# Low-rank layers and preparation of the recurrence moved beside the convolved projection; layer 1's modulation moved into the first feed-forward

## The reference

```python
cs = silu(c)
for l in range(2):
    mod = cs @ ada_w[l] + ada_b[l]          # 1024 x 6144: shifts, scales, gates of layer l
    h = rmsnorm(x, g) * (1 + sc1) + sh1
    if l == 0:
        z = h @ mix_in                      # 4*512 columns r, k, v, u and 3*512 of the attention
        r, k, v, u = split(dwconv3(z[..., :2048], mix_conv))
        g = sigmoid(u @ g1) @ g2
        kk = k * k_k;  kk = kk * rsqrt(sum(kk*kk, per head) + eps)
        for d in range(2):                  # two directions
            w = decay(w0[d] + tanh(u @ w1[d]) @ w2[d])
            a = sigmoid(a0[d] + (u @ a1[d]) @ a2[d])
            kd = k * (1 + (a - 1) * k_a)
            y += wkv7_scan(r, w, kd, v, kk, a)
            bonus += sum(r * kd * r_k, per head) * v
    ...
    h = rmsnorm(x) * (1 + sc2) + sh2
    y = (gelu(gate) * val) @ down           # gate, val = split(dwconv3(h @ up)), 2 * 2816 columns
```

## Time and profile before

| | |
|---|---|
| median of 3 runs | 3074.9 us (3071.58 to 3075.23) |
| profiled execution, its own time | 3071.72 us |
| its span, first to last instruction | 3069.9 us |
| PE busy | 2658.7 us, 87% of the span |
| DVE busy | 1577.3 us, 51% |
| ACT busy | 1129.5 us, 37% |
| POOL busy | 979.2 us, 32% |

### The profile page before, as it was taken

One profiled execution on the slowest core, in us unless ns is written; L12 is line 12 of the kernel. 1 busy time (PEld: TensorE's weight loads), 2 busy tenths in 40 slices (PEclk: granted clock), 3 DMA queues, 4 the chain that ended last, 5 costly groups with the idle time before them and its releaser, 6 DMA issues. The chain is left out here.

```text
span 3069.9 us, 55055 instructions
## 1 busy us (share of the span) xinstructions
PE 2658.7 (87%) x23104; PEld 2154.1 (70%) x23104; DVE 1577.3 (51%) x2253; ACT 1129.5 (37%) x1774; POOL 979.2 (32%) x660
## 2 busy tenths in 40 slices
PE   2698997965789989558899999999778899999998
PEld 1576775731789889347688888877556688888887
DVE  4463664503555454416555556445626555556445
ACT  2211224523434333224344444445324344444434
POOL 0411111003212111142577775000131577775000
PEclk9799998987899999769899999999879899999999
DMA  4555745046311310332222223754032222223654
GB/s 167 161 179 175 240 171 149 16 148 245 93 44 47 83 44 4 117 118 83 70 84 85 85 83 131 245 170 148 30 96 83 75 88 85 83 83 135 236 187 143
DMA packets 301852, 361.14 MB, mean 118 GB/s; under 512 B 31652, under 2 KB 227585, under 8 KB 301613
## 3 DMA queue, kind: packets, MB, share of 16 engines
q1 hardware_dynamic: 291966, 351.38, 35.1%
q10 hardware_dynamic: 9648, 6.34, 0.6%
HBM read 282.12 MB, written 75.55 MB: 117 GB/s over the span
## 5 line engine op out<-in xcount | busy, mean ns | idle before, releaser
L2401 POOL TENSOR_TENSOR cg_u_lo<-cg_u_raw,cg_u_hi 128x512 fp32r<-128x512 f32 x216 | 329.3, 1533 | 136.4 <-ACT cg_u_hi L2287 136.4
L304 PE MATMUL cg_ps<-m_hi,cg_u_hi 128*128 128x512 f32 x844 | 331.3, 393 | 33.0 <-POOL cg_u_lo L2401 28.7
L306 PE MATMUL cg_ps<-m_hi,cg_u_lo 128*128 128x512 f32 x844 | 330.8, 392 | 0.0
L305 PE MATMUL cg_ps<-m_lo,cg_u_hi 128*128 128x512 f32 x808 | 316.0, 391 | 0.0
L2287 ACT ACTIVATE cg_u_hi<-cg_u_raw 128x512 fp32r<-128x512 f32 x216 | 132.1, 629 | 386.5 <-PE cg_ps L306 234.1
L304 PEld LDWEIGHTS cg_ps<-m_hi,cg_u_hi 128*128 128x128 f32 x844 | 159.9, 189 | 68.2 <-POOL cg_u_lo L2401 29.5
L304 PE MATMUL cg_ps<-over_y_tx,cg_u_hi 128*128 128x512 f32 x480 | 186.7, 389 | 0.0
L305 PE MATMUL cg_ps<-over_y_tx,cg_u_hi 128*128 128x512 f32 x480 | 186.7, 389 | 0.0
L306 PE MATMUL cg_ps<-over_y_tx,cg_u_lo 128*128 128x512 f32 x480 | 186.7, 389 | 0.0
L306 PEld LDWEIGHTS cg_ps<-m_hi,cg_u_lo 128*128 128x128 f32 x844 | 159.7, 189 | 33.6
L2451 DVE SCALAR_TENSOR_TENSOR cg_z<-cg_ps,top_conv_f,cg_z 128x1023 f32<-128x1023 f32 x88 | 112.9, 1283 | 133.8 <-ACT cg_z L2311 133.8
(11 more groups left out here) (416 smaller groups left out, 6691.8 us busy)
## 6 DMA issues: line engine op xcount, KB each, us to landing
cg_u_raw<-in_ffn_up SPq DMA_DIRECT2D x88, 512.0 KB, 5.3
cg_u_raw<-in_ffn_down SPq DMA_DIRECT2D x64, 512.0 KB
za_mw<-in_ada_w SPq DMA_DIRECT2D x12, 2048.0 KB
over_f_d_raw<-in_ffn_down SPq DMA_DIRECT2D x48, 512.0 KB
scr_act<-cg_z SPq DMA_DIRECT2D x44, 512.0 KB, 2.7
qkv_mw<-in_ada_w SPq DMA_DIRECT2D x8, 2048.0 KB
mod_w<-in_ada_w SPq DMA_DIRECT2D x8, 1024.0 KB
za_w_raw<-in_mix_in SPq DMA_DIRECT2D x16, 512.0 KB, 4.3
```

The lines of the kernel that those rows point to most:

```text
L304: nc.tensor.matmul(out, a_hi, b_hi, start=first, stop=False)
L305: nc.tensor.matmul(out, a_hi, b_lo, start=False, stop=False)
L306: return nc.tensor.matmul(out, a_lo, b_hi, start=False, stop=last)
L2401: G.tensor_tensor(u_lo[:, n % RING], source(g, i), u_hi[:, n % RING].bitcast(F32), ALU.subtract).then_inc(ulo_done, 1)
```

## The change

`project_convolved` becomes `project_and_prepare`. It makes the tiles in the order u0..u3, k0..k3, r0, v0, r1, v1, r2, v2, r3, v3, keeps them in SBUF, and between the tiles runs what the two low-rank stages did, on a pair of PSUM buffers `pr` that the small products take in turn (`ORDER`). Both low-rank stages and their loads from DRAM are gone; the stores of z and of the results stay. Two weight buffers are left of four. The loops are written out.

```diff
-            project_convolved(nc, a["mix_in"], consts["conv_a"], h_hi, h_lo, scr["z"], a["ada_w"], a["ada_b"], scr["mod"], consts)
+            project_and_prepare(nc, a["mix_in"], consts["conv_a"], h_hi, h_lo, a["rwkv_w1"], a["rwkv_a1"], a["rwkv_g1"], a["rwkv_w2"],
+                                a["rwkv_a2"], a["rwkv_g2"], tab, consts, scr["z"], scr["lw"], scr["aa"], scr["kk"], scr["bon"],
+                                scr["gate"], scr["vr"])
...
-            with ExitStack() as lctx:
-                ls = Scope(nc, lctx, "lh")
-                tw, ta, tg = (ls.sb(n, [P, S]) for n in ("tw", "ta", "tg"))
-                lora_hidden(nc, scr["z"], a["rwkv_w1"], a["rwkv_a1"], a["rwkv_g1"], tw, ta, tg)
-                prepare_recurrence(nc, scr["z"], a["rwkv_w2"], a["rwkv_a2"], a["rwkv_g2"], tab, consts, tw, ta, tg, scr["lw"], scr["aa"],
-                                   scr["kk"], scr["bon"], scr["gate"], scr["vr"])
```

```diff
+        def pair_of(c):
+            return PLAIN + 1 + 3 * c // 2
...
+                for c in range(MC):
+                    if g == (pair_of(c - 1) if c else PLAIN):
+                        load_chunk(c)
...
                     gelu(g - 1)
+                    for c in range(MC):
+                        if g == pair_of(c) + 1:
+                            chunk_out(c)
                     for i in range(2, 5):
                         ahead(n + i + RING)
...
+                    chunk_rows(g, range(0, KT // 2))
                     dve.wait_ge(umm_done, n + 4)
...
                     convolve(g, VAL)
+                    chunk_rows(g, range(KT // 2, KT))
                     dve.wait_ge(umm_done, n + 6)
...
                 times(bank(g, VAL, 0), n + 4, *of_t(3)).then_inc(umm_done, 1)
+                for c in range(MC):
+                    if g == pair_of(c) + 1:
+                        pe.wait_ge(ms.acc_done, c + 1)
+                        if c:
+                            pe.wait_ge(ms.row_done, c)
+                        ms.add_up(0, 0)
```

More of the change, by code:

```diff
@@ L623, in chunk_out @@
[L623 to L635, removed]
-                        split(i + 1, 0)
-                    middle(i, j)
-                    if j >= 2:
-                        chunk_out(i, j - 2)
-                chunk_out(i, CI - 1)
@@ new lines, in middle @@
+            def middle(p):
+                kind, f = divmod(TILES[p], KU)
+                act.wait_ge(mm_done, p + 1)
+                if kind == R and f >= 2:
+                    act.wait_ge(r_stored[f % 2], 16 * (f // 2))
+                    act.wait_ge(bonus_in, f - 1)
+                if kind == V and f >= 2:
+                    act.wait_ge(v_stored[f % 2], 16 * (f // 2))
+                    read(act, f"H{f - 2}")
+                A(place(p), ps[:, p % 2, :], ACT.Copy, scale=conv_cols[:, 1, TILES[p]:TILES[p] + 1]).then_inc(mid_done, 1)
@@ new lines, in _ @@
+            split(0)
+            split(1)
+            for p in range(5):
+                step(p)
+            hidden(0, tw, ACT.Tanh)
+            step(5)
+            hidden(1, ta, ACT.Copy)
+            step(6)
+            hidden(2, tg, ACT.Sigmoid)
+            key(0)
+            key(1)
+            step(7)
+            sigmoids(0, 0, W0)
+            squares(0)
+            squares(1)
+            key(2)
+            key(3)
+            step(8)
+            sigmoids(0, 2, A0)
+            gated(0)
@@ new lines, in _ @@
+            squares(2)
+            squares(3)
+            act.wait_ge(eps_set, 1)
+            read(act, "S3")
+            A(root[:, :], root[:, :], ACT.Sqrt, bias=eps[:, 0:1]).then_inc(root_in, 1)
+            rate(0)
+            step(9)
+            sigmoids(1, 0, W0)
+            sigmoids(1, 2, A0)
+            reverse(0)
+            step(10)
+            gated(1)
+            rate(1)
+            step(11)
+            sigmoids(2, 0, W0)
+            reverse(1)
+            step(12)
+            sigmoids(2, 2, A0)
@@ new lines, in times_key @@
+            def times_key(f):
+                pool.wait_ge(rated, f + 1)
+                G.tensor_tensor(both[:, f % 2, :], both[:, f % 2, :], kt[:, f, :], ALU.mult).then_inc(rated_k, 1)
+            for p in range(11):
+                low(p)
+            sum_rates(0)
+            times_key(0)
+            low(11)
+            sum_rates(1)
+            low(12)
+            times_key(1)
+            low(13)
+            low(14)
+            sum_rates(2)
+            times_key(2)
+            low(15)
@@ new lines, in _ @@
+            X.reciprocal(root[:, :], root[:, :]).then_inc(root_done, 1)
+            bonus_of(0)
+            convolve(9)
+            convolve(10)
+            bonus(0)
+            unit(0)
+            unit(1)
+            bonus_of(1)
+            convolve(11)
+            unit(2)
+            convolve(12)
+            bonus(1)
+            unit(3)
+            bonus_of(2)
+            convolve(13)
+            convolve(14)
+            bonus(2)
+            bonus_of(3)
+            convolve(15)
```

703 lines of the change are left out of this document (386 added, 317 removed).

## The result

The changed kernel takes 3143.84 us (median of 4 runs, 3142.58 to 3146.26) against 3073.58 for the kernel before (median of 4, 3071.58 to 3075.23): ratio 1.023, 95% interval 1.0212 to 1.0248. It is slower by 70 us, where 3130 was forecast. Its profiled execution took 3143.44 us. The experiments were timed in three groups, and the kernel before beside them took 3073.91, 3074.43 and 3070.76 us; each ratio is to the kernel before of its own group.

What follows compares the result with a forecast made beforehand. PE was taken as the bound in the projection and the feed-forward's up part. 3069.9 - 59.8 + 105.6 + 11 = 3126.7 us of span, 3128.5 profiled, forecast as 3130; range 3068 to 3160, likeliest case 3100 to 3155.

Steps and rivals of the forecast that it cites:

- Removed, and the projection: Low-rank stages gone, -123.6 us; their work added to the projection stage, +63.8; together -59.8.
- Idle time of the small products: Projection: between tiles, small products wait for ACT to read a `pr` buffer, 8.5 us in all.
- the clock: Feed-forward: PE partly at half clock after some 18 waits, 0.6 us each, +11 us; bounds 0 and 49.
- the tail: Projection's end: a bonus product or reversal after the taps, about +1.2 us, and two more stores, +0.3.
- Rows only: Feed-forward pair with DVE rows but no sum: rows and POOL delay each other, PE gets product 4 4.5 us late.
- The sum's wait: Feed-forward: ACT waits for PE's sum before splitting product 6; PE idle 3.2 us, 3.65 in a pair with both.
- the feed-forward's two terms: Up part of the first feed-forward: +105.6 us for 12 modulation chunks, and +11 for lost clock.
- the two mechanisms: Feed-forward: ACT's wait for the sum and DVE's rows competing with POOL both cost; 3100 to 3155 us, chance 0.58.
- a pair with both: Feed-forward pair with rows and a sum: 8.2 us, including later PE waits of 0.3, 1.3 and 2.0.
- Rows that slip between POOL's instructions: Rival, feed-forward: DVE's rows fit into POOL's idle time; 3079 us, range 3067 to 3092, chance 0.17.
- the sum that costs only its 1.0: Rival, feed-forward: ACT's wait costs PE nothing, only 12 sums of 1.0 stay; 3024 us, chance 0.10.
- The late loads: Part of the slower rival, feed-forward: odd chunks' loads come 2 to 4 us late, +18; 3150 to 3170, chance 0.15.

Runs made afterwards that it cites:

- e10_modulation_only: The kernel before, with only its layer 1 modulation moved into the first feed-forward as the change does: 3186.33 us, ratio 1.0362.
- e2_one_row: The changed kernel with only the first of each chunk's eight DVE rows computed, seven left out: 3082.71 us, ratio 1.0025 to the kernel before.
- e4_psum_rows: The changed kernel with rows 2 to 8 of each chunk added in the sum's PSUM bank: 3096.22 us, ratio 1.0069 to the kernel before.
- e1_sum_early: The changed kernel with PE's sum moved from behind product 5 to behind product 3: 3082.06 us, ratio 1.0027 to the kernel before.
- e6_filler: The changed kernel with three unused float32 matmuls behind each of the 12 sums: 3136.26 us, ratio 1.0204 to the kernel before.
- e7_all_three: The changed kernel with sum behind product 3, rows 2 to 8 in PSUM, rows' second half behind the gate's outer taps: 3073.31 us, ratio 0.9998.

## Why the prediction was right, point by point

- **Removed, and the projection.** -59.8 forecast, -58.3 measured. From PE's first matmul of the stage to the attention's first issue it is 541.88 - 276.16 = 265.7 us, before 475.76 - 278.52 = 197.2: +68.5 for +63.8. Idle time of the small products was 9.9 for 8.5: behind tile 9 the rates waited 3.8 in place of 2.5. ACT loads its function table anew between a root and the next sigmoid (1.28 us at 425.30), a step that the sum lacked: the two sigmoids follow it until 428.71, PE goes on at 428.86, and 2.5 + 1.3 is the wait.

  The larger miss is the clock, which the prediction counted in the feed-forward and at nothing here, without a reason. From the rates at 428.86 to the end of tile 10 it is 14.4 us, from the roots at 464.72 to the end of tile 12 16.2, and for such a product with its tile at full clock 13.0 (487.79 to 500.81): 4.6 us lost. The granted clock was 0.79 from 428 to 436 us and 0.69 from 468 to 476. In `e10_modulation_only`, where only the 12 sums leave the stage, it is 13.3 us shorter for the -12 forecast. These, 1.4 + 4.6 - 1.3, come to the miss of 4.7; what else differs (the tail +2.6 for +1.5, the small products about as much less) cancels out. The rows are PE's first of the stage, after and before, the two slow products, and ACT's load of the table:

```profile
276.16 0.79 PE L307 MATMUL za_ps<-h_hi,za_w_hi 128*128 128x512 f32 x1 [11.43 <-POOL za_w_lo L983]
...
425.30 1.28 ACT L907 ACT_TABLE_LOAD   x1
426.59 2.12 ACT L907 ACTIVATE za_out<-za_pr,top_vec 128x1024 f32<-128x1024 f32 x2
...
428.86 3.50 PE L781 MATMUL za_pr<-za_ta,za_a2s 64*128 64x512 f32 x8 [3.76 <-ACT za_out L907]
...
464.72 2.46 PE L756 MATMUL za_pr<-za_root,za_spread 32*128 32x512 f32 x4 [1.24 <-ACT za_out L907]
```

```profile
278.52 0.80 PE L304 MATMUL za_ps<-h_hi,za_w_hi 128*128 128x512 f32 x1 [11.29 <-POOL za_w_lo L657]
```

  Against this the stage began 2.4 us earlier (276.16 for 278.52; 275.36 in `e10_modulation_only`, so this comes with the modulation's leaving and not with the new stage), the attention took 0.85 less. These two were not forecast and brought the sum back near the mark: that it came out within 1.5 us is partly luck.
- **Rows only.** This pair runs as worked out. ACT's copy of product 1 is at 1563.72, so product 1 began at 1560.9. The first four rows end at 17.0 (16.9 forecast), the outer taps at 22.7 (22.9), the later four at 26.2 (26.4), POOL at 31.2 (31.6). Behind it PE waited 0.30 and 3.37 for a forecast 4.5. That these rows cost something on the path is shown by `e2_one_row`, and that it is their length beside POOL by `e4_psum_rows`.
- **The sum's wait.** Copy, split, subtraction: 3.00 twice a three, for 3.2 and 3.65 forecast. `e1_sum_early` shows that it is the place of the sum behind product 5, and that moving it is worth 61.8 us, 5.15 a sum.
- **The failed term: the clock.** +11 was taken, 1.8 a three, of bounds 0 and 49. In the rows of PE above, the five waits of a three are 0.30 + 3.37 + 3.00 + 0.96 + 3.00 = 10.6, for 15.6 forecast. Two sums are 2.4 (14.7 / 12 each). The rest of the 21.3, 8.3 us, is PE's own slowness: between 1592.12 and 1599.38 two products take 7.26 for 5.44, between 1603.39 and 1620.19 five take 16.8 for 13.6. A record of 0.39 takes 0.63 there, the level of 1.2 GHz. Six times 8.3 is 50, the upper bound: 18 waits of 3 us or more at 2.8 us each. The 0.6 us a wait of the forecast came from a stretch cut at 2119, while PE was still slow. In the same trace the records stay at 0.63 until 2121.1:

```profile
2120.68 0.63 PE L306 MATMUL cg_ps<-m_hi,cg_u_lo 128*128 128x512 f32 x1
2121.11 0.47 PE L304 MATMUL cg_ps<-over_f_d_hi,cg_a_hi 128*128 128x512 f32 x1
```

  The 12 matmuls from 2116.77 on took 4.34 us for 2.72, so the row, read to its end, says 1.6 a wait and +29. The rest up to 50 is that the slow stretches of the changed kernel were longer still. The rule quoted from the Trainium skill, "TensorE: Matmul & The Clock Gate", section "HAM oscillation — how this bites in real kernels", said that each such gap brings half clock anew, and as an account of PE's time the trace agrees with it behind 3.37 and both 3.00. In the projection the clock fell behind one wait of 1.24 us too (at 464.72, with small products ahead of it), and not behind the four other waits of that length.
- **As a price it was not that.** With the clock at 0.97, `e6_filler` is only 7.6 us faster, though all its fillers lie inside waits (3.00 becomes 2.79 of filler and 0.28 of waiting). The forecast took wait and clock as apart; they share one gap. ACT, POOL and DVE decide when weights are there, and a slow PE arrives late and waits less: the clock took 6.5 more a three than the forecast had, the waits 5.0 less. What stays is 21.3 for 19.4 a three, 128 for 116.6: the feed-forward's two terms together were 11 us too small, and the forecast's mean and this miss are the same 11 us and 3 more (3144 for 3130).
- **How the two mechanisms combine.** In the expectations each alone was worth less (32 and 46 us) than half of both (117), since the other's waits would stay. Measured, they are 61.8 and 61.1 alone and 111.5 together: almost independent. That fits a pair with both in which the later waits (0.96 for 1.3 + 0.3 + 2.0 forecast) were overstated; the runs don't take that pair apart further.
- **The rivals.** Rows that slip between POOL's instructions: against it stands 1.75 for each of the first four. Against the sum that costs only its 1.0 stands `e1_sum_early`. The late loads did not come in the changed kernel (DVE's first rows waited for PE's sum, 24.4 us in five waits from 1485 to 1880, never for DMA; the load issued at 1587.21 had 13.3 us until its rows began), but came at once in `e7_all_three`.
- **The median.** The profiled execution is 0.4 us under the median. The 3.2 us that the forecast took from the kernel before were 1.9 once its fourth run was in (3073.58). The forecast's 1.8 around the span was right (3143.44 - 3141.7 = 1.7).

## What to carry to other kernels

Work that fits an engine's idle share still has to fit its queue: here ACT was busy for 31% of the stretch, and one 0.6 us copy that waits for a sum, put ahead of three splits, cost 5 us each time. Put such a copy behind a producer that ends early, two products sooner, and only the sum's own 1.2 us stay. Give work that shares DVE with a busy POOL a PSUM input where it can have one. With a single buffer, the last read of a chunk is the start of the next load: whoever moves that read must count the load's time anew, or load in halves. And don't add a lost clock to the waits that cause it: if another engine sets the pace, both are parts of one gap. Where a slow clock is to be priced from a row, follow the records to where they are fast again.

## What the runs showed of the hardware

- DVE's multiply-add of 128x512 with two SBUF inputs took 0.75 alone and 1.74 while POOL worked, and POOL's subtractions stretched too (1.27 to 1.73 in the rows around 1603 us). With one input in PSUM it took 744 to 757 ns in 72 of 72.
- Products on 64 rows of the array's two halves overlapped by plan, as they had by chance before, here one call of four matmuls (eight records) in 1.99 us with its drain, for 1.83 worked out:

```profile
386.69 1.99 PE L781 MATMUL za_pr<-za_tw,za_w2s 64*128 64x512 f32 x8
```

- The 2 MB load of a chunk in the feed-forward took 9.0 us from its issue to the first row that waited for it (1575.11 to 1584.15), beside the weight loads.
